# Half of an output projection computed in 32 steps among the steps of the samples' attention

## The chip, the core and the metric

One core of one Trainium2 chip. The time is device microseconds of one execution, median of three. The engines are PE (TensorE; PEld is its weight load), ACT (ScalarE), DVE (VectorE), POOL (GpSimd) and SP (SyncE, which here only issues DMAs). Each runs its own list of instructions in order, and they wait for each other on semaphores.

## The reference

One layer for 512 prompt tokens (one sequence) and 64 sample tokens (8 samples of 8 new tokens, each over 2048 cached positions). Attention has three branches, each with its own K and V; a short gated convolution stands beside it. Cut to what matters here:

```python
q, kv_c, kv_s, kv_w, gates, xin, bg, cg = in_projection(x, w_in)
attn = nsa_attention(...)         # gates0*o_cmp + gates1*o_sel + gates2*o_win
conv_out, conv_state = short_conv(xin, bg, cg, conv_prev, conv_w)
mix = concatenate([attn, conv_out]) @ w_out          # 2048 x 2048
h = layer_norm(ALPHA * x + mix, ln1_g, ln1_b)
f = square(relu(h @ w_mlp1)) @ w_mlp2
y = layer_norm(ALPHA * h + f, ln2_g, ln2_b)
```

The products with `w_out` are wanted for all 576 tokens. A token's row of `mix` depends on that token alone, so prompt tokens can be projected before the samples' attention is done.

## The kernel before

Activations lie transposed: 16 tiles of 128 features by T = 576 tokens, in two halves of TH = 288. The first half holds the prompt tokens 0 to 287, the second the other prompt tokens and the 64 sample tokens. The order of all work is written out by hand, engine by engine.

A float32 product is made of three passes: each operand is split into a high part (ACT's copy to `F32R`) and a low part (DVE's subtraction), and PE adds high x high, high x low and low x high. So one 128x128 block of a weight against one half of the tokens costs three matmuls of 288 columns.

The stages around the change, in order of time:

- the prompt's attention, up to about 795 us.
- The samples' attention, 795 to 993 us, one step for each of 8 samples. For sample b the cached K/V rows of the selected branch come in two gathers of 2 MB (`sg`, issued by POOL, one descriptor of 16 KB for each row), those of the window in one load of 1 MB (`wb`, SP). There are six chunks of keys: 0 and 1 in the first gather, 2 and 3 in the second, 4 the window, 5 the new tokens. `k_turn` transposes a chunk on PE, ACT copies it to `kT` (L914), `k_qk` makes the scores (L2257, chunk 5 L2259), DVE adds the mask (L1525, L1529) and takes the maxima (L1540). While the keys of sample b are worked on, sample b-1 is finished: ACT's exponentials (`s_exp`, L919), DVE's scaling (L1558), transposes of the weights (`s_turn`, L2270), ACT's copy to `sT` (L929), products with V (`s_pvs`, L2292), and `o_turn` (L2299) with DVE's addition to `mix`. A buffer of `sg` may be refilled when its products with V are done; there are four. There are two `kT`.
- The output projection, 996 to 1214 us, in two passes over the same weights. Pass 0 is for the first half of the tokens, pass 1 for the second. In each pass, for each of the 16 output tiles, SP loads a 1 MB weight tile (five DMAs), ACT makes its high part (L794), DVE its low part (L799), PE runs 48 matmuls (`gemm_half`, L2344), and DVE adds the residual from `x_scratch` (`residual`, L1613 and L1615) and adds up the sum for the layer norm. The tokens' own splits are made ahead of pass 0 for both halves (L969, L1604), tile by tile, and the first `gemm_half` waits for each.
- Beside pass 1, the layer norm of the first half; then the MLP.

## Time and profile before

| | |
|---|---|
| median of 3 runs | 2720.15 us (2719.93, 2720.15, 2726.3) |
| profiled execution, span from first to last instruction | 2725.8 us |
| PE busy | 2605.0 us, 96% of the span |
| DVE busy | 2001.9 us, 73% |
| ACT busy | 1073.5 us, 39% |
| HBM read and written | 385.53 MB and 96.80 MB |

### The profile page before, as it was taken

Reading aid. Unit: us, or ns where it says so; the run is one execution under the profiler, and the core shown is the slowest. Engines: PE = TensorE matmul, PEld = TensorE weight load, DVE = VectorE, ACT = ScalarE, POOL = GpSimd, SP = SyncE. Lnnn points to the kernel's source line nnn. Section 1 sums busy time; section 2 is a strip of 40 time slices with the busy share of each in tenths; the row PEclk is TensorE's granted clock in tenths of the full one; section 3 lists DMA queues with packets and bytes.
Section 4 is the critical chain, followed back from the end, with each engine's and each line's share of the span. In section 5 each row is a group of like instructions: output and inputs, shape, how many; then the busy total and the mean of one; then the engine's idle time right before and its main releaser. Section 6 shows DMA issues by size and latency. Waiting matters only on the chain.

```text
span 2725.8 us, 52530 instructions
## 1 busy us (share of the span) xinstructions
PE 2605.0 (96%) x20061; PEld 2482.8 (91%) x20061; DVE 2001.9 (73%) x3169; ACT 1073.5 (39%) x1349; POOL 66.6 (2%) x118
## 2 busy tenths in 40 slices
PE   8999999998888889996999999999999999999998
PEld 8999999995556569996999999999999999999997
DVE  5778732326864455689888888888888888888898
ACT  3111111116764453455555555555533333333333
POOL 1000000000001100000000000000000000000001
PEclk9999999998999999998999999999999999999999
DMA  8776643316025547653555555555796556555642
GB/s 263 229 242 209 184 77 77 87 39 236 2 94 221 210 135 210 197 157 116 190 188 194 193 192 189 185 190 190 255 321 190 180 168 209 184 186 177 201 125 85
DMA packets 510464, 475.35 MB, mean 174 GB/s; under 512 B 48957, under 2 KB 460885, under 8 KB 499447
## 3 DMA queue, kind: packets, MB, share of 16 engines
q1 hardware_dynamic: 505306, 406.85, 47.7%
q0 software_dynamic: 4736, 67.18, 6.5%
q8 instruction: 59, 0.97, 0.2%
q14 instruction: 31, 0.25, 0.0%
q10 hardware_dynamic: 332, 0.11, 0.0%
HBM read 385.53 MB, written 96.80 MB: 177 GB/s over the span
## 4 chain that ended last, share of the span: by engine, by line
PE 63%; DVE 5%; DMA 3%; issue 2%; ACT 2%; SPq 1%; DVEq 0%; ACTq 0%; POOL 0%; POOLq 0%
PE ps L2432 49%; PE ps L2344 6%; PE ps L2292 1%; DMA sg<-in_cache_slc,idx 1%; PE ps L2191 1%; PE ps L2244 1%; PE ps L2181 1%; DMA f_b<-f_scratch 1%; DVE pS L1473 1%; PE ps L2257 1%; PE ps L2270 1%; PE ps L2205 1%; DVE o_rows L1987 0%; DVE w_sl L1630 0%; ACT pT L895 0%
## 5 line engine op out<-in xcount | busy, mean ns | idle before, releaser
L1027 ACT ACTIVATE w_sh<-w_s 128x1024 fp32r<-128x1024 f32 (+1 forms) x512 | 473.5, 949 | 785.5 <-PE ps L2432 522.2
L2432 PE MATMUL ps<-f_b,w_sh 128*128 128x288 f32 x3584 | 714.5, 296 | 10.1 <-DMA f_b<-f_scratch 7.7
L1630 DVE TENSOR_TENSOR w_sl<-w_s,w_sh 128x1024 fp32r<-128x1024 f32 (+1 forms) x512 | 554.7, 1089 | 124.3 <-ACT w_sh L1027 124.1
L2432 PEld LDWEIGHTS ps<-f_b,w_sh 128*128 128x128 f32 x3584 | 574.2, 189 | 13.4 <-DMA f_b<-f_scratch 7.5
L2432 PE MATMUL ps<-f_b,w_sl 128*128 128x288 f32 x1792 | 527.0, 294 | 0.0
L2432 PE MATMUL ps<-h_u,w_sh 128*128 128x288 f32 x2560 | 514.3, 296 | 11.4 <-DVE h_u L1770 10.9
L2432 PEld LDWEIGHTS ps<-h_u,w_sh 128*128 128x128 f32 x2560 | 411.1, 189 | 12.9 <-issue 6.8
L2432 PE MATMUL ps<-h_u,w_sl 128*128 128x288 f32 x1280 | 376.7, 294 | 0.0
L794 ACT ACTIVATE w_hi<-w_raw 128x2048 fp32r<-128x2048 f32 x77 | 147.6, 1917 | 554.3 <-PE ps L2032 466.3
L2432 PEld LDWEIGHTS ps<-f_b,w_sl 128*128 128x128 f32 x1792 | 338.9, 189 | 0.0
L2032 PE MATMUL ps<-x_hi,w_hi 128*128 128x288 f32 x1408 | 302.6, 297 | 0.0
L2032 PE MATMUL ps<-x_hi,w_lo 128*128 128x288 f32 x1408 | 301.2, 296 | 0.0
L2032 PE MATMUL ps<-x_lo,w_hi 128*128 128x288 f32 x1408 | 300.9, 295 | 0.0
L2432 PEld LDWEIGHTS ps<-h_u,w_sl 128*128 128x128 f32 x1280 | 242.5, 189 | 0.0
L2032 PEld LDWEIGHTS ps<-x_hi,w_lo 128*128 128x128 f32 x1408 | 226.5, 189 | 0.0
L2032 PEld LDWEIGHTS ps<-x_lo,w_hi 128*128 128x128 f32 x1408 | 226.5, 189 | 0.0
L2032 PEld LDWEIGHTS ps<-x_hi,w_hi 128*128 128x128 f32 x1408 | 226.3, 189 | 0.1
L2432 PE MATMUL ps<-h_a,w_sh 128*128 128x288 f32 x1024 | 208.4, 296 | 13.5 <-DVE w_sl L1630 13.5
L799 DVE TENSOR_TENSOR w_lo<-w_raw,w_hi 128x2048 fp32r<-128x2048 f32 x77 | 176.6, 2293 | 60.6 <-ACT w_hi L794 58.8
L1882 DVE TENSOR_TENSOR y_t<-y_t,ps 128x288 f32 (+1 forms) x416 | 182.7, 450 | 45.5 <-PE ps L2432 43.2
L2344 PE MATMUL ps<-mixs,w_hi 128*128 128x288 f32 x1024 | 208.7, 299 | 5.3 <-DVE mixs L1604 3.2
L2432 PEld LDWEIGHTS ps<-h_a,w_sh 128*128 128x128 f32 x1024 | 164.8, 189 | 13.8 <-DVE w_sl L1630 13.7
(302 smaller groups left out, 3153.1 us busy)
## 6 DMA issues: line engine op xcount, KB each, us to landing
w_s<-in_w_mlp SPq DMA_DIRECT2D x512, 256.0 KB, 3.7
f_scratch<-f_st SPq DMA_DIRECT2D x32, 2016.0 KB, 8.9
f_b<-f_scratch SPq DMA_DIRECT2D x56, 1152.0 KB, 8.3
w_raw<-in_w_in SPq DMA_DIRECT2D x90, 512.0 KB, 5.1
w_raw<-in_w_out SPq DMA_DIRECT2D x128, 128.0 KB, 2.9
w_raw<-in_w_out SPq DMA_DIRECT2D x32, 512.0 KB, 4.3
x_r<-x_scratch SPq DMA_DIRECT2D x32, 288.0 KB, 4.4
wb<-in_cache_win SPq DMA_DIRECT2D x8, 1024.0 KB, 7.6
```

Source lines behind the costliest of these rows:

```text
L794: nc.scalar.activation(w_hi[s % 2][:, :], w_raw[s % 2][:, :], ACT.Copy).then_inc(s_hi, 1)
L799: nc.vector.tensor_tensor(w_lo[s % 2][:, :], w_raw[s % 2][:, :], w_hi[s % 2][:, :].bitcast(F32), ALU.subtract).then_inc(s_lo, 1)
L1027: nc.scalar.activation(w_sh[m][:, :, :], blocks, ACT.Copy).then_inc(z_h[m], 1)
L1473: last = nc.vector.tensor_tensor_reduce(pS[u % 4][:, br, 0:n], ps[:, 2 * (u % 2) + br, 0:n], causal[:, TP - n:TP], -1.0, 3e38, ALU.add, AL ...
L1630: nc.vector.tensor_tensor(w_sl[m][:, :, :], blocks, w_sh[m][:, :, :].bitcast(F32), ALU.subtract).then_inc(z_l[m], 1)
L1882: nc.vector.tensor_tensor(view, view, ps[:, bank, 0:TH], ALU.add).then_inc(z_e[m], 1)
L2032: last = nc.tensor.matmul(out[:, h, :], w[:, k * P:(k + 1) * P], x[:, k, h * TH:(h + 1) * TH], start=(k == 0 and m == 0), stop=(k == KT - ...
L2181: last = nc.tensor.matmul(ps[:, 2 * gl + br, 0:n], pq[a][half, n - P:n], kv_t[half, kv + a, 0:n], start=True, stop=True)
L2191: last = nc.tensor.transpose(ps[:, 4 + x // 4, (x % 4) * P:(x % 4 + 1) * P], pS[u % 4][:, br, kt * P:(kt + 1) * P], ident[:, :])
L2205: last = nc.tensor.matmul(ps[gl * HD:(gl + 1) * HD, 6 + a, i * P:(i + 1) * P], kvn[:, kt, v0:v0 + HD], pT[(2 * j + gl + 16 * r) % 3][:, x, ...
L2344: last = nc.tensor.matmul(ps[:, 2 * (s % 2), 0:TH], w[:, k * P:(k + 1) * P], mixs[:, p, x, k, :], start=(k == 0 and m == 0), stop=(k == KT ...
L2432: last = nc.tensor.matmul(ps[:, bank, 0:TH], w[b][:, at_, cols], acts(k, x), start=(start and n == 0), stop=(stop and n == 2), skip_group_ ...
```

## The change

Pass 0 is taken out of the projection and cut into 32 parts (`e_part`, `e_step`), which stand on PE among the steps of the samples' attention. Part e belongs to output tile e // 2. Even parts take the 8 feature tiles of the convolution, odd parts the 8 of the attention, so a part is 24 matmuls of 288 columns, and the weight comes in half tiles of 512 KB (`e_load`: one DMA for an even part, four for an odd one), with its own splits (`e_split` on ACT, `e_low` on DVE, 128x1024 each). Two parts stand in step 0, four in each of the steps 1 to 7, two behind them. The result of a tile (with the residual, `e_residual`) goes to memory (`c_scratch`, `e_store`), and before the layer norm it is read back into `h_t` in four DMAs. The splits of the first half of the tokens (`mix_high`, `mix_low`, 4 pieces of 128x1152) are made in step 0; those of the second half stay behind the attention. Pass 1 keeps its 16 tiles of 48 matmuls.

To make room, `sg` has three buffers where there were four, and `kT` and its two banks of PSUM are single where they were double. From sample 1 on the chunks come in the order 0, 1, 4, 2, 3, 5. The loops over samples are written out.

The core of the diff:

```diff
-S_OUT2 = S_OUT + KT
-S_MLP = S_OUT2 + KT
+S_MLP = S_OUT + KT
...
+NE = 2 * KT
+E_FIRST = (0,) + tuple(2 + 4 * n for n in range(NB))
+FIRST_CHUNKS, CHUNKS = (0, 1, 2, 3, 4, 5), (0, 1, 4, 2, 3, 5)
...
+        m_hi = at("m_hi", X0, [P, KT, TH], F32R)
+        m_lo = at("m_lo", C0, [P, KT, T], F32R)
+        sg = [at(f"sg{i}", X0 + HB + 16384 * ((i + 1) % 3), [P, GROW, ROWW]) for i in range(3)]
+        assert X0 + HB + 3 * 16384 <= B0
...
+        kT = at("kT", B0 + 14400, [P, 2, 512])
+        e_xr = at("e_xr", B0 + 18496, [P, 2, TH])
+        sT = [at(f"sT{i}", B0 + 22592 + 2048 * i, [P, 4, P]) for i in range(3)]
...
+            def e_load(e):
+                n, dst = slice(e // 2 * P, e // 2 * P + P), e_raw[e % 2]
+                if e >= 2:
+                    sp.wait_ge(e_los, e - 1)
+                if e % 2 == 0:
+                    sp.dma_start(dst[:, :].rearrange("p (k n) -> p k n", n=P), w_cnv_v[:, :, n]).then_inc(e_w[0], 16)
+                else:
+                    for a in range(2):
+                        for gl in range(2):
+                            sp.dma_start(dst[gl * HD:(gl + 1) * HD, :].rearrange("p (r a n) -> p r a n", r=R, a=2)[:, :, a, :],
+                                         w_att_v[a, gl][:, :, n]).then_inc(e_w[1], 16)
+            def e_load_x(n):
+                if n:
+                    sp.wait_ge(e_tile, 32 * n)
+                    sp.wait_ge(l_sum, 1 + n)
+                sp.dma_start(e_xr[:, :, :], x_dram[:, n, :, 0:TH]).then_inc(e_tile, 16)
+            def e_store(n):
+                sp.wait_ge(e_acc, 2 * n + 2)
+                sp.dma_start(c_dram[:, n, :], e_xr[:, 0, :]).then_inc(e_tile, 16)
+            sp.wait_ge(s_xsave, 16 * 2 * KT // 4)
+            e_load(0)
+            e_load(1)
+            load_window(0)
+            e_load_x(0)
+            load_window(1)
+            e_load(2)
+            e_load(3)
+            for b in range(1, NB):
...
+                e = E_FIRST[b]
+                e_load(e + 2)
+                e_store(e // 2 - 1)
+                e_load_x(e // 2)
+                e_load(e + 3)
+                e_load(e + 4)
+                e_store(e // 2)
+                e_load(e + 5)
+                e_load_x(e // 2 + 1)
+                if b + 1 < NB:
+                    load_window(b + 1)
...
+            e_store(KT - 1)
+            load(S_OUT + 2, out_loads(S_OUT + 2, 1, 0))
+            load_x(2, 0)
+            sp.wait_ge(e_tile, 32 * KT)
+            sp.wait_ge(s_mlo, 4 + KT)
+            sp.wait_ge(e_mm, NE)
+            for q in range(4):
+                sp.dma_start(h_t[:, 4 * q:4 * q + 4, 0:TH], c_dram[:, 4 * q:4 * q + 4, :]).then_inc(e_tile, 16)
+            load(S_OUT + 3, out_loads(S_OUT + 3, 1, 1))
+            load_x(3, 0)
...
+            def seq_gather(m):
+                if m >= 3:
+                    pool.wait_ge(t_pv, 6 * ((m - 3) // 2) + 2 * ((m - 3) % 2) + 2)
+                nc.gpsimd.tensor_copy(idx1[m % 4][:, :], idx[:, m:m + 1]).then_inc(s_idx1, 1)
+                pool.wait_ge(s_idx1, 2 * NGATH + 2 * m + 1)
+                pool.sem_inc(s_idx1, 1)
+                nc.gpsimd.indirect_dma_start(
+                    sg[m % 3][:, :, :].rearrange("p j c -> p (j c)"), None, slc_rows,
+                    bass.IndirectOffsetOnAxis(ap=idx1[m % 4][:, 0:1], axis=0)).then_inc(s_sg[m % 3], 16)
...
+            def e_split(e):
+                act.wait_ge(e_w[e % 2], (64 if e % 2 else 16) * (e // 2 + 1))
+                if e >= 2:
+                    act.wait_ge(e_mm, e - 1)
+                nc.scalar.activation(e_high(e)[:, :], e_raw[e % 2][:, :], ACT.Copy).then_inc(e_his, 1)
...
+            mix_high(0)
+            k_copy(0, 0)
+            mix_high(1)
+            k_copy(0, 1)
+            mix_high(2)
+            e_split(0)
+            k_copy(0, 2)
+            mix_high(3)
+            e_split(1)
+            k_copy(0, 3)
+            k_copy(0, 4)
+            e_split(2)
+            e_split(3)
+            for b in range(1, NB):
+                e = E_FIRST[b]
+                k_copy(b, 0)
+                s_exp(b - 1)
+                k_copy(b, 1)
+                e_split(e + 2)
+                for g in range(3):
+                    p_copy(b - 1, g)
+                k_copy(b, 2)
+                e_split(e + 3)
+                p_copy(b - 1, 3)
+                p_copy(b - 1, 4)
+                k_copy(b, 3)
+                if b < NB - 1:
+                    e_split(e + 4)
+                    e_split(e + 5)
+                k_copy(b, 4)
+                p_copy(b - 1, 5)
+                if b == NB - 1:
+                    e_split(e + 4)
+                    e_split(e + 5)
+                o_copy(b - 1)
...
+            def e_low(e):
+                dve.wait_ge(e_his, e + 1)
+                nc.vector.tensor_tensor(e_lo[e % 2][:, :], e_raw[e % 2][:, :], e_high(e)[:, :].bitcast(F32), ALU.subtract).then_inc(e_los, 1)
+            def e_residual(n):
+                dve.wait_ge(e_mm, 2 * n + 2)
+                dve.wait_ge(e_tile, 32 * n + 16)
+                nc.vector.scalar_tensor_tensor(e_xr[:, 0, :], e_xr[:, 0, :], ALPHA, ps[:, 2 + n % 2, 0:TH], ALU.mult, ALU.add).then_inc(e_acc, 1)
+                dve.wait_ge(e_acc, 2 * n + 1)
+                nc.vector.scalar_tensor_tensor(e_xr[:, 0, :], e_xr[:, 1, :], ALPHA, e_xr[:, 0, :], ALU.mult, ALU.add).then_inc(e_acc, 1)
+                dve.wait_ge(e_acc, 2 * n + 2)
+                dve.wait_ge(l_sum, n + 1)
+                nc.vector.tensor_tensor(h_sum[:, 0:TH], h_sum[:, 0:TH], e_xr[:, 0, :], ALU.add).then_inc(l_sum, 1)
...
+            mix_low(0)
+            mix_low(1)
+            k_scores(0, 0)
+            mix_low(2)
+            k_scores(0, 1)
+            mix_low(3)
+            e_low(0)
+            k_scores(0, 2)
+            e_low(1)
+            k_scores(0, 3)
+            k_scores(0, 4)
+            k_scores(0, 5)
+            k_max(0)
+            e_low(2)
+            e_residual(0)
+            for b in range(1, NB):
+                e = E_FIRST[b]
+                if b > 1:
+                    s_out_add(b - 2)
+                e_low(e + 1)
+                s_scale(b - 1)
+                k_scores(b, 0)
+                k_scores(b, 1)
+                e_low(e + 2)
+                k_scores(b, 2)
+                e_residual(e // 2)
+                e_low(e + 3)
+                k_scores(b, 3)
+                if b < NB - 1:
+                    e_low(e + 4)
+                k_scores(b, 4)
+                k_scores(b, 5)
+                k_max(b)
+                if b == NB - 1:
+                    e_low(e + 4)
+                e_residual(e // 2 + 1)
...
+            def e_part(e, j0, j1):
+                n, kh = e // 2, e % 2
+                if j0 == 0:
+                    pe.wait_ge(e_los, e + 1)
+                    if kh == 0 and n >= 2:
+                        pe.wait_ge(e_acc, 2 * n - 3)
+                    if n == 0:
+                        pe.wait_ge(s_mlo, 2 * kh + 2)
+                for j in range(j0, j1):
+                    k, cols = j if kh else NCONV + j, slice(j * P, (j + 1) * P)
+                    hi, lo = e_high(e)[:, cols], e_lo[e % 2][:, cols]
+                    for m, (w, x) in enumerate(((hi, m_hi[:, k, :]), (hi, m_lo[:, k, 0:TH]), (lo, m_hi[:, k, :]))):
+                        last = nc.tensor.matmul(ps[:, 2 + n % 2, 0:TH], w, x, start=(kh == 0 and j == 0 and m == 0),
+                                                stop=(kh == 1 and j == 7 and m == 2))
+                if j1 == 8:
+                    last.then_inc(e_mm, 1)
...
+            k_turn(0, 0)
+            k_turn(0, 1)
+            k_qk(0, 0)
+            k_turn(0, 2)
+            k_qk(0, 1)
+            e_step(0)
+            k_turn(0, 3)
+            k_qk(0, 2)
+            e_step(1)
+            k_turn(0, 4)
+            k_qk(0, 3)
+            k_qk(0, 4)
+            k_qk(0, 5)
+            for b in range(1, NB):
+                e = E_FIRST[b]
+                k_turn(b, 0)
+                if b > 1:
+                    o_turn(b - 2)
+                e_step(e)
+                k_qk(b, 0)
+                k_turn(b, 1)
+                s_turn(b - 1, 0)
+                s_turn(b - 1, 1)
+                k_qk(b, 1)
+                s_pvs(b - 1, 0)
+                s_turn(b - 1, 2)
+                s_pvs(b - 1, 1)
+                k_turn(b, 2)
+                e_step(e + 1)
+                k_qk(b, 2)
+                s_turn(b - 1, 3)
+                s_pvs(b - 1, 2)
+                s_turn(b - 1, 4)
+                s_pvs(b - 1, 3)
+                e_step(e + 2)
+                k_turn(b, 3)
+                e_step(e + 3)
+                k_qk(b, 3)
+                k_turn(b, 4)
+                s_turn(b - 1, 5)
+                s_pvs(b - 1, 4)
+                k_qk(b, 4)
+                s_pvs(b - 1, 5)
+                k_qk(b, 5)
+            o_turn(NB - 2)
+            e_step(NE - 2)
+            for g in range(6):
+                s_turn(NB - 1, g)
+                if g:
+                    s_pvs(NB - 1, g - 1)
+            s_pvs(NB - 1, 5)
+            e_part(NE - 1, 0, 4)
+            o_turn(NB - 1)
+            e_part(NE - 1, 4, 8)
...
-            for u in range(2):
-                gemm_half(S_OUT + u, 0, 0, ready=True)
-            with pe.Fori(1, KT // 2) as i:
-                for u in range(2):
-                    gemm_half(S_OUT + u, 2 * i, 0)
+            pe.wait_ge(e_acc, 2 * KT - 3)
             for i in range(8):
-                gemm_half(S_OUT2 + i, 0, 1)
+                gemm_half(S_OUT + i, 0, ready=i < 1)
```

ACT in the later part of a middle step of the attention, before. `kT` is the copy of transposed keys, `sT` that of transposed weights of the sample before, `o_sb` its result:

```order
L914 ACTIVATE kT_137<-ps 128x1024
L926 REGISTER_ALU
L929 ACTIVATE sT<-ps 128x512
L926 REGISTER_ALU
L929 ACTIVATE sT<-ps 128x512
L911 REGISTER_ALU
L912 REGISTER_ALU
L914 ACTIVATE kT_138<-ps 128x1024
L925 REGISTER_ALU
L926 REGISTER_ALU
L931 ACTIVATE sT<-ps 8x256
L936 ACTIVATE o_sb_144<-ps 128x128
```

The same part of a step in the changed kernel. `e_hi` is the high part of a half tile of `w_out`:

```order
L993 ACTIVATE kT<-ps 128x1024
L986 ACTIVATE e_hi_144<-e_raw_142 128x1024
L1012 ACTIVATE sT_138<-ps 128x512
L1012 ACTIVATE sT_139<-ps 128x512
L993 ACTIVATE kT<-ps 128x1024
L986 ACTIVATE e_hi_143<-e_raw_141 128x1024
L986 ACTIVATE e_hi_144<-e_raw_142 128x1024
L993 ACTIVATE kT<-ps 128x1024
L1014 ACTIVATE sT_140<-ps 8x256
L1019 ACTIVATE o_sb_154<-ps 128x128
```

The copies come in the order they had, with splits of weights between them, each of which waits for its own load; the last two stand ahead of the last `kT`. One more split stands earlier in the step, ahead of the first `sT`.

SP in the same step, before: one window and its two rows of new V, nothing else.

```order
L503 DMA wb_132<-in_cache_win 128x2048
L506 ISA
L506 DMA vn_136<-out 8x256
L506 ISA
L506 DMA vn_136<-out 8x256
```

And now, from the first half tile of a step to the next window:

```order
L535 DMA e_raw_141<-in_w_out 128x8x128
L552 DMA c_scratch<-e_xr 128x288
L547 DMA e_xr<-x_scratch 128x2x288
L539 DMA e_raw_142<-in_w_out 64x4x128 x4
L535 DMA e_raw_141<-in_w_out 128x8x128
L552 DMA c_scratch<-e_xr 128x288
L539 DMA e_raw_142<-in_w_out 64x4x128 x4
L547 DMA e_xr<-x_scratch 128x2x288
L525 DMA wb_130<-in_cache_win 128x2048
```

Every store waits for DVE's residual, every load of `e_xr` for the store ahead of it to land, and the window for the last product with V of the sample two before it.

## Rows read from the trace of the kernel before

**Rows 1.** The page, whole execution: span, and TensorE (busy, share, instructions).
```profile
span 2725.8 us, 52530 instructions
...
PE 2605.0 (96%) x20061; PEld 2482.8 (91%) x20061; DVE 2001.9 (73%) x3169; ACT 1073.5 (39%) x1349; POOL 66.6 (2%) x118
```

**Rows 2.** Busy time by stretch: PE, PEld, DVE, ACT, POOL, PEclk, DMA share, GB/s.
```profile
795.00:811.00 16.00, 11.80 (x76) 6.67 (x72) 7.71 (x17) 5.01 (x5) 3.39 (x7) 0.92 0.83 313
811.00:835.00 24.00, 21.68 (x178) 14.86 (x178) 9.11 (x23) 10.96 (x15) 2.52 (x5) 0.91 0.50 196
...
931.00:955.00 24.00, 21.68 (x183) 14.92 (x179) 10.35 (x30) 11.23 (x16) 2.45 (x5) 0.93 0.57 216
955.00:975.00 20.00, 15.92 (x107) 10.40 (x105) 10.65 (x30) 9.38 (x13) 0.00 (x0) 0.91 0.26 100
975.00:996.00 21.00, 15.45 (x194) 11.63 (x188) 7.39 (x23) 11.75 (x20) 0.00 (x0) 1.00 0.21 57
```

**Rows 3.** The chain of waits in one sample step: start us, us, what.
```profile
885.11 1.72 PE ps L2244 x8
...
887.85 1.07 ACT sS L919
...
894.14 1.02 PE ps L2292 x16
895.17 1.02 PE ps L2244 x8
896.19 1.01 PE ps L2257 x4
...
904.70 0.70 DVE sS L1529
...
905.52 1.05 PE ps L2259 x8
```

**Rows 4.** Busy time around that step's start, granted clock after POOL's column.
```profile
880.00:883.00 3.00, 2.11 (x20) 1.38 (x16) 1.63 (x5) 0.00 (x0) 0.21 (x1) 1.00 0.90 360
883.00:887.00 4.00, 4.00 (x23) 3.49 (x21) 1.28 (x7) 1.37 (x3) 0.19 (x1) 0.57 0.98 367
887.00:907.00 20.00, 17.68 (x162) 11.25 (x158) 9.11 (x23) 9.86 (x14) 2.53 (x5) 1.00 0.52 190
```

**Rows 5.** Timeline after a group of transposes, with the idle time before the next group.
```profile
896.12 0.20 PEld L2257 LDWEIGHTS ps<-kT,qb 128*64 128x64 f32 x4 [0.17 <-issue]
```

**Rows 6.** Products of the projection alone (L2344): PE, PEld, clock, DMA, GB/s.
```profile
996.00:1008.40 12.40, 10.64 (x49) 8.20 (x49) 0.86 0.86 231
1008.40:1105.00 96.60, 96.17 (x719) 95.94 (x720) 1.00 0.74 209
```

**Rows 7.** Groups of instructions by line, projection and attention stretch.
```profile
L914 ACT ACTIVATE kT<-ps 128x1024 f32<-128x1024 f32 x40 | 40.8, 1022 | 48.8 <-PE ps L2244 48.8
...
L1613 DVE SCALAR_TENSOR_TENSOR h_t<-x_r,ps 128x288 f32 x16 | 7.3, 454 | 30.5 <-PE ps L2344 30.5
```

**Rows 8.** The same view of the MLP stretch, for tiles of the new sizes.
```profile
L1630 DVE TENSOR_TENSOR w_sl<-w_s,w_sh 128x1024 fp32r<-128x1024 f32 x383 | 468.1, 1222 | 115.4 <-ACT w_sh L1027 115.2
...
L1027 ACT ACTIVATE w_sh<-w_s 128x1024 fp32r<-128x1024 f32 x383 | 403.4, 1054 | 381.0 <-DVE w_s L1653 252.6 <-PE ps L2432 120.4 <-DVE w_s L1635 5.5
...
L1770 DVE TENSOR_TENSOR h_u<-h_r,h_u 128x1152 fp32r<-128x1152 f32 x8 | 10.9, 1358 | 2.5 <-ACT h_u L1079 1.7
...
L1079 ACT ACTIVATE h_u<-h_r 128x1152 fp32r<-128x1152 f32 x8 | 9.3, 1164 | 16.2 <-DVE h_r L1762 16.2
```

**Rows 9.** DMA queues from 36 to 40 us: packets, MB, share of 16 engines.
```profile
q0 software_dynamic: 104, 1.70, 100.1%
q1 hardware_dynamic: 36, 0.01, 1.3%
```

**Rows 10.** Landing times of the two w_raw loads issued at 29.1 and 29.5.
```profile
DMA to landing us min/median/max: 5.4/10.0/14.6
```

**Rows 11.** The selection gathers (tile sg), 16 of them.
```profile
DMA to landing us min/median/max: 8.1/9.2/19.2
```

**Rows 12.** DMA issues of the output projection, KB each, median us to landing.
```profile
w_raw<-in_w_out SPq DMA_DIRECT2D x31, 512.0 KB, 4.3
```

More of the change, by code:

```diff
@@ L396, in build @@
         z_f = [sem(f"z_f{m}") for m in range(7)]
-        o_tr, o_cp = sem("o_tr"), [sem(f"o_cp{i}") for i in range(2)]
+        o_tr, o_cp = sem("o_tr"), sem("o_cp")
         s_dve, s_pool = sem("s_dve"), sem("s_pool")
@@ L542, in _ @@
                     sp.wait_ge(s_acc, 2 + S_OUT + n + 1 - XR + XR * i)
-                    load_x(n, i, 0)
-            with sp.Fori(0, KT // XR) as i:
-                for n in range(XR):
-                    load(S_OUT2 + n, out_loads(S_OUT2 + n, 2 * i + n // 2, n % 2), it=XR * i)
-                    sp.wait_ge(s_acc, 2 + S_OUT2 + n + 1 - XR + XR * i)
-                    load_x(n, i, 1)
+                    load_x(n, i)
             w1_v = w_mlp1[0].rearrange("(c k a p) n -> p c a k n", p=P, a=2, k=CK)
@@ L774, in _ @@
+            seq_gather(0)
+            seq_gather(1)
             pool.wait_ge(s_pv, 2 + UNITS)
             pool.wait_ge(s_of, 2 + 2 * R)
-            seq_q(0, 0)
-            seq_q(1, 0)
-            seq_gather(1, 0)
-            with pool.Fori(1, NB // 2) as i:
-                for h in range(2):
-                    seq_q(h, i)
-                    seq_gather(h, i)
+            seq_q(0)
+            seq_q(1)
+            seq_gather(2)
+            for b in range(1, NB):
+                seq_gather(2 * b + 1)
+                if b + 1 < NB:
+                    seq_gather(2 * b + 2)
+                    seq_q(b + 1)
@@ new lines, in _ @@
+            s_exp(NB - 1)
+            p_copy(NB - 1, 0)
+            p_copy(NB - 1, 1)
+            p_copy(NB - 1, 2)
+            act.wait_ge(e_los, NE)
+            split_hi(act, S_OUT)
+            for g in range(3, 6):
+                p_copy(NB - 1, g)
+            o_copy(NB - 1)
+            act.wait_ge(t_of, NB)
+            for k in range(0, KT, 2):
+                nc.scalar.activation(mixs[:, 0, k:k + 2, :], mix[:, k:k + 2, TH:T], ACT.Copy).then_inc(s_mhi, 2)
+            act.wait_ge(e_mm, NE)
@@ new lines, in _ @@
+            s_out_add(NB - 2)
+            e_low(NE - 1)
+            s_scale(NB - 1)
+            split_lo(dve, S_OUT)
+            s_out_add(NB - 1)
+            for k in range(0, KT, 2):
+                if k == 8:
+                    e_residual(KT - 1)
+                dve.wait_ge(s_mhi, 4 + k + 2)
+                nc.vector.tensor_tensor(mixs[:, 1, k:k + 2, :], mix[:, k:k + 2, TH:T], mixs[:, 0, k:k + 2, :].bitcast(F32),
+                                        ALU.subtract).then_inc(s_mlo, 2)
@@ L2208, in p_pv @@
                             last.then_inc(s_pv, 1)
-            for first in (t_qk, t_pv, t_pt):
-                pe.sem_inc(first, 12)
             pe.sem_inc(s_qk, 1)
```

377 lines of the change are left out of this document (150 added, 227 removed).

## The prediction

> **What bounds the kernel now.** I read the page first: PE is busy for 2605.0 of 2725.8 us [rows 1]. All matmuls that pass 0 needs are still run, so nothing shortens PE's own work: the change can only put products where PE stands idle. The busy times by stretch [rows 2] say where that is. The samples' attention goes from 795 to 996 us; its first step takes 16.0 us with PE busy for 11.8, the next six 24.0 us each with PE busy for 21.7 (the first and the last of them are shown; DVE has 9 to 10 and ACT 11 of the 24), and the last two stretches 41.0 us with 31.4. That is 4 + 14 + 10 = 28 us of idle PE, the most that the parts could fill there. Next I read the chain of one such step [rows 3]. It is mostly PE, with short links through ACT and DVE: the exponentials (1.07 on the chain), the window's scores (0.70). Two groups of 8 transposes take 1.72 us at its start, and the same group takes 1.02 later [rows 3]. The busy times around them say why: the granted clock is 0.57 over 4 us, so 1.2 GHz for about 3.4 of them, after 3 us in which PE was busy for 2.1; then it is back at 1.00 [rows 4]. This costs 2 x 0.7 = 1.4 us in each step. So a step is 24.0 = 20.3 of work, 1.4 of clock, 2.3 of waits. The last view is that of the products alone [rows 6]: 720 in 96.6 us, 0.134 each, and the first 48 in 12.4 us instead of 6.4, since they wait for the splits of the tokens.
>
> **What moves, and its break-even.** A part is 24 x 0.134 = 3.2 us of PE, the four of a step 12.9. Pass 0 shrinks by exactly that. So a middle step must take less than 24.0 + 12.9 = 36.9 us, or the move costs.
>
> **Middle steps (1 to 6).** PE: 20.3 + 12.9, and each part is one more group with a join. A join shows as 0.17 us of idle PEld between two groups whose operands are long there [rows 5]; I take 0.15, so 0.6 for four. Sum 33.8. On top of it:
> - Clock. What stands at the end of a step is what stood there before: the last scores of 512 columns, the scores of the new keys, the short products, and a wait. I take it that the clock falls as it did. But now a dense part stands behind it, so half speed for 3.4 us costs 1.7 instead of 1.4. Bounds: 0, if the parts keep the clock up, and 3.4, if it falls twice.
> - Waits. DVE gets four `e_low` of 1.22 [rows 8] and six instructions of 0.46 [rows 7], 7.6 us, to its 10; ACT four splits of 1.05, 4.2 us, to its 11. Both stay under 20 of 37 us and cost nothing by their sum. What costs is the order on ACT, where a split waits for a load and copies that PE needs stand behind it. The loads are pieces of 512 bytes, and gathers of 16 KB pieces run beside them in every step. Where they met before, the gather took the DMA engines: in 4 us 104 packets with 1.70 MB of its queue, and 36 packets with 0.01 MB of the other [rows 9]; the load issued 1 us ahead of two gathers landed after 14.6 us, its neighbour after 5.4 [rows 10]. Now the fourth load of a step (`e_load(e + 5)`) is issued about 22 us into the step, when DVE has made the low part ahead of it, and the second gather is asked for at the same place, after the fourth product with V. A gather lands after 9.2 us [rows 11], and about 1 us passes before it is issued, so both are there at about 33. ACT then splits (1.05) and copies `kT` (1.02 [rows 7]): about 35.2. PE, with the clock's 1.7, wants that copy at 33.8 + 1.7 - 2.7 = 32.8. A wait of 2.4. This takes the place of the 2.3 that the step had, which the parts do fill. Bounds: 0.5 (load ahead of the gather) to 8 (another of the loads stands behind a gather too).
> - The gather with three buffers. Between the product with V that frees a buffer and the chunk that needs it PE has two groups of keys, two of scores and products with transposes and two parts, 3.4 each, in all 11.6 us (groups of 1.02 and transposes of four at half of that [rows 3]); the gather needs 1 + 9.2: hidden, with 1.4 to spare. Above 10.6 us of landing it shows; the slowest took 19.2 [rows 11], beside other traffic.
>
> So 33.8 + 1.7 + 2.4 = 37.9 against 36.9: +1.0, six times, **+6.0**.
>
> On this the Trainium skill has two rules. "TensorE: Matmul & The Clock Gate", section "Loop structure matters more than you think": matmuls that stand back to back stay warm. Rows 4 show only that the clock fell behind thinner work; by the rule the parts would hold it up, and a step would be 36.2, a saving of 0.7. "DMA: Bandwidth & Descriptors", section "Queues, rings and completion order": a DMA engine takes the queues in turn, by packets. Rows 9 agree, and the rule speaks against the change: with pieces of 512 bytes against 16 KB a turn each is next to nothing, and it holds for every load that meets a gather.
>
> **Step 0.** Before, 16.0 us [rows 2]. Now ACT has the four splits of the tokens (1.16 each, DVE's half 1.36 [rows 8]) and two of weights among its copies, and the first part waits for them. By the order: ACT three token splits, two `kT` and the first weight split, 3 x 1.16 + 2 x 1.02 + 1.05 = 6.6; then `kT` 1.02 and the last token split 1.16; DVE 1.36 and 1.22; part 0, 3.2; two groups of PE, 2.0; scores and maximum, 1.4; the second `e_low` 1.22; part 1, 3.2; two groups, 2.0; the only `kT`, 1.0; the last scores, 1.0 + 0.7 + 1.05. That is 29.1 us, with some fifteen links of 0.1 30.6, and I take 31, since the first half tiles are loaded beside a gather and two windows. Bounds: 28, and 36. 31 - 16.0 - 6.4 = **+8.6**. This is the step that speaks most against the change: two parts bring 6.4 us of work into a step of 16 and lengthen it by 15.
>
> **The end.** Before, 41.0 us from the last sample's keys to the first product [rows 2]. Now step 7: 33.8 + 1.7 + 0.5, as there is no next gather. Then part 30 (3.4), which hides the exponentials but not DVE's scaling (some 3 more), six pairs of transposes and products with V (9.0), part 31 (3.2), and the splits of the second half (1.4): 20.0. Together 56.0, less six parts (19.3) 36.7: **-4.3**. The first tile of pass 1: its token splits are in pieces half as large in all, DVE's 8 x 0.75 and a residual, so about 9.0 instead of 12.4: **-3.4**. Then the way back from memory: 2.36 MB are read ahead of the fourth weight tile. In the projection 209 GB/s are moved at a share of 0.74 [rows 6], so 282 at the most: 8.4 us for it and 3.7 for each 1 MB tile. From the last store, about 7 us into pass 1: 3.7 + 8.4 + 3.7 and both splits (4.2) is 27; the fourth tile's products are due at 9.0 + 2 x 6.4 = 21.9. **+5.4**; bounds 0 and 10. A tile alone lands in 4.3 [rows 12], so the later ones catch up. Sum of the end: -2.3. Storing and loading the tiles in the steps costs PE nothing more; SP waits there, not PE.
>
> **Sum.** 8.6 + 6.0 - 2.3 = +12.3 us. Against the profiled execution that is 2725.8 + 12.3 = 2738.1 of span; against the median, 5.65 lower, 2720.15 + 12.3 = **2732**.
>
> **The rivals.**
> - A: faster. The parts keep the clock up and the late load comes in time: a step is 33.8 + 0.5 = 34.3, -2.6 six times, -15.6; step 0 at 29.5, +7.1; the end without clock and with half of the wait for memory, -2.3 - 1.7 - 2.7 = -6.7. Sum -15: 2705. For it: idle of 2.3 in each step is there to fill, and DVE and ACT have room. Against it: rows 9 and 10.
> - B: no difference that can be told. Only one of the two holds. Clock up, load late: 36.2, -0.7 six times, -4.2, + 8.6 - 4.0 = 0: 2720. Load in time and the clock down: 36.0, -5.4 + 8.6 - 2.3 = +1: 2721.
> - C: much slower. Each of the loads that stand ahead of copies meets a gather, above all the second of a step, ahead of the fourth `sT`, and slows the gather in turn beyond its 1.4 us to spare. A step of 33.8 + 1.7 + 7 = 42.5, +5.6 six times, 33.6 + 8.6 - 2.3 = +40: 2760. It decides from the point where the load of part e + 3 lands later than about 18 us into the step. For it: rows 10. Against it: this load is issued some 3 us before the first gather is.
> - D: the change does nothing: parts stand in PE's list beside the waits, not in them. 24.0 + 12.9 + 0.6 = 37.5, +3.6 + 8.6 - 2.3 = +10: 2730. It can't be told from the forecast by time, only by the waits before `kT` and `sT`.
>
> **How the numbers follow.** A run of this kernel tells about 0.3% from no change, 8.2 us: below 2712.0 is faster, above 2728.3 slower. Chances: forecast and D together 0.42 (2724 to 2741), A 0.18, B 0.24, C 0.16. Of the forecast's case a tenth of the chance, 0.04, falls within 0.3%; of A one in six, 0.03, does; of B 0.03 lies above. Faster 0.16, the same 0.27, slower 0.57. The range leaves out the far half of A and of C: 2705 to 2758; the likeliest case alone 2724 to 2741. The sum has no term that could be large and favourable at once: idle PE is 28 us in all, and the clock takes 9 more.
>
> **What would show it.** Step 0 of 31 us, with the first part waiting for a low part of DVE. Middle steps of 37.9 with one wait of 2 to 3 us ahead of the last 512-column scores, released by `kT`, and that by the split of the fourth half tile, and that by its DMA, landing after 8 us or more while others take 4 to 5. The granted clock at half once in a step. 12.9 us less of pass 0 for each. The fourth tile of pass 1 late by 5 us. I am wrong if middle steps are under 36 us, or if the clock stays at 1.00 through the attention.

## The result and the profile after

The changed kernel takes 2761.43 us (median of 4, 2759.07 to 2762.6), the kernel before 2722.52 (median of 4, 2719.93 to 2726.3). The ratio is 1.0137, 95% interval 1.0122 to 1.0151: slower by 39 us, where 12 were forecast. The time lies 3 us above the range of 2705 to 2758.

The page's first lines, of the profiled execution (2760.63 us; they answer to [rows 1]):

```profile
span 2758.8 us, 51737 instructions
...
PE 2626.6 (95%) x20061; PEld 2500.7 (91%) x20061; DVE 2005.2 (73%) x3181; ACT 1072.8 (39%) x1361; POOL 70.2 (3%) x118
```

The span is 33 us longer and PE is busy for 21.6 of them, with the same 20061 matmuls: some of them run slower. The busy times by stretch, as in [rows 2] (step 0, steps 1, 2 and 5, then step 7 and the end):

```profile
795.00:831.20 36.20, 23.66 (x119) 16.66 (x117) 15.82 (x18) 13.11 (x13) 2.60 (x4) 0.79 0.54 183
831.20:872.10 40.90, 37.26 (x275) 29.20 (x276) 18.70 (x38) 15.02 (x20) 3.19 (x5) 0.88 0.56 178
872.10:913.80 41.70, 37.30 (x277) 29.68 (x277) 18.10 (x39) 15.01 (x20) 3.18 (x5) 0.87 0.63 200
995.80:1036.50 40.70, 36.88 (x276) 29.25 (x277) 18.10 (x39) 15.02 (x20) 3.18 (x5) 0.88 0.63 204
1077.10:1133.30 56.20, 52.50 (x436) 43.51 (x436) 28.13 (x67) 24.59 (x35) 1.14 (x2) 0.92 0.46 144
```

A middle step is 41.0 us (246.0 for six), where 36.9 would break even. DVE and ACT are busy for 18 and 15 of them, so neither is the bound. The mean clock fell to 0.88, where [rows 2] have 0.91 to 0.93. The budget against the forecast, each difference net of the parts moved (24 x 0.134 = 3.22 us each); the numbers taken off are the stretch before (15.8 and 143.9 us) and the parts:

| | forecast | measured |
|---|---|---|
| step 0 | +8.6 | 36.1 - 15.8 - 6.4 = +13.9 |
| steps 1 to 6 | +6.0 | 246.0 - 143.9 - 77.2 = +24.9 |
| the end, up to the MLP | -2.3 | -1.9 |
| ahead of step 0 and after the MLP's start | 0 | -3.7 |
| sum | +12.3 | +33 |

What gave the last 3.7 us back was not looked into.

The chain of waits at the end of step 4 (start us, us, what) names the wait:

```profile
976.38 1.15 DVE e_lo L1628
...
979.51 9.55 DMA e_raw<-in_w_out
...
989.20 0.85 issue
990.05 1.01 ACT kT L993
991.06 0.04 issue
991.11 1.97 PE ps L2401 x4
993.08 1.05 PE ps L2441 x8
994.13 1.81 PE ps L2403 x8
995.93 1.80 PE ps L2385 x8
```

This is the forecast's chain link by link: DVE's low part, the load of `e_load(e + 5)`, ACT's split (the 0.85 of "issue" are its first part), the `kT` copy, and PE. The instructions of SP, ACT and POOL there, and what ended ACT's idle time:

```profile
977.54 2.59 SPq L539 DMA_DIRECT2D e_raw<-in_w_out  x4
...
978.37 0.96 POOL L834 DMA_INDIRECT sg<-in_cache_slc,idx  x1 [0.81 <-POOLq L833]
...
989.09 1.06 ACT L986 ACTIVATE e_hi<-e_raw 128x1024 fp32r<-128x1024 f32 x1 [6.02 <-DMA e_raw<-in_w_out]
990.05 1.00 ACT L993 ACTIVATE kT<-ps 128x1024 f32<-128x1024 f32 x1
```

Then the groups in the chain take too long: eight transposes 1.80 us against the 1.02 of [rows 3], the 512-column scores 1.97 against 1.01. The busy times around them, granted clock third from the end:

```profile
986.00:990.00 4.00, 1.50 (x21) 1.02 (x19) 1.82 (x2) 0.91 (x1) 0.00 (x0) 1.00 0.55 129
990.00:1000.30 10.30, 9.19 (x40) 7.26 (x41) 4.92 (x14) 4.12 (x6) 0.00 (x0) 0.50 0.50 156
1000.30:1008.00 7.70, 7.02 (x56) 4.78 (x55) 5.83 (x16) 4.13 (x8) 0.00 (x0) 1.00 0.44 123
```

The clock is at its lower level, 1.2 GHz, for 10.3 us, where [rows 4] have it there for 3.4. All six middle steps have such a stretch of 10.2. What it costs, from start to start of the groups against the same groups at full clock: scores 1.90 against 1.01, short products 1.05 against 0.86, the new keys' scores 1.73 against 0.91, transposes 1.74 against 0.91, the first part 4.80 against 3.34. That is 0.89 + 0.19 + 0.82 + 0.83 + 1.46 = 4.2 us a step. At the wait itself two matmuls start 3.2 to 4.0 us apart (3.5 in the mean of the six steps), which start 0.15 apart where nothing is waited for: 3.3 more. Together 7.5 us a step.

### The profile page after: what moved, and what is told of

It is laid out like the page before. It is cut to its first block, busy times and chain, and to the rows that moved or that the text cites. A ratio compares the mean times of both kernels' runs of the same rounds, so it can differ in the third digit from the quotient of the medians.

```text
span 2758.8 us, 51737 instructions
## 1 busy us (share of the span) xinstructions
PE 2626.6 (95%) x20061; PEld 2500.7 (91%) x20061; DVE 2005.2 (73%) x3181; ACT 1072.8 (39%) x1361; POOL 70.2 (3%) x118
## 4 chain that ended last, share of the span: by engine, by line
PE 62%; DVE 6%; DMA 3%; ACT 3%; issue 2%; SPq 1%; DVEq 0%; ACTq 0%
PE ps L2620 49%; PE ps L2536 3%; PE ps L2463 3%; DMA e_raw<-in_w_out 2%; PE ps L2401 1%; PE ps L2331 1%; PE ps L2385 1%; PE ps L2441 1%; PE ps L2321 1%; DVE pS L1575 1%; PE ps L2345 1%; DMA f_b<-f_scratch 1%; PE ps L2403 0%; DVE o_rows L2127 0%; DVE w_sl L1775 0%
## 5 line engine op out<-in xcount | busy, mean ns | idle before, releaser
L2620 PE MATMUL ps<-h_u,w_sh 128*128 128x288 f32 x2560 | 516.3, 297 | 10.3 <-DVE h_u L1910 9.9
L861 ACT ACTIVATE w_hi<-w_raw 128x2048 fp32r<-128x2048 f32 x61 | 116.8, 1915 | 483.9 <-PE ps L2172 466.3
L866 DVE TENSOR_TENSOR w_lo<-w_raw,w_hi 128x2048 fp32r<-128x2048 f32 x61 | 139.9, 2294 | 53.2 <-ACT w_hi L861 51.4
L1786 DVE TENSOR_TENSOR w_s<-w_s 128x1024 f32<-128x1024 f32 x128 | 156.5, 1223 | 2.3
```

What stands on the lines that cost most here:

```text
L861: nc.scalar.activation(w_hi[s % 2][:, :], w_raw[s % 2][:, :], ACT.Copy).then_inc(s_hi, 1)
L866: nc.vector.tensor_tensor(w_lo[s % 2][:, :], w_raw[s % 2][:, :], w_hi[s % 2][:, :].bitcast(F32), ALU.subtract).then_inc(s_lo, 1)
L1786: nc.vector.tensor_tensor(w_s[:, b + 2:SUM_2 + 1:SUM_2 - b - 2, :], w_s[:, b + 2:SUM_1 + 1:SUM_1 - b - 2, :], w_s[:, b:b + 1, :].broadcast ...
L2620: last = nc.tensor.matmul(ps[:, bank, 0:TH], w[b][:, at_, cols], acts(k, x), start=(start and n == 0), stop=(stop and n == 2), skip_group_ ...
```

## The experiments

The theory after this: one late load per step makes one wait, and that wait, through the clock, costs twice its length. Its rivals: the clock falls because of what PE does at a step's end, whatever it waits for; the load is late for some reason other than the gather. In each expectation "1, 2, 3" are its own theories.

**The late split moved.** In steps 1 to 6:

```diff
                 if b < NB - 1:
                     e_split(e + 4)
-                    e_split(e + 5)
                 k_copy(b, 4)
...
                 o_copy(b - 1)
+                if b < NB - 1:
+                    e_split(e + 5)
```

> ACT's split of the fourth half tile (e + 5) stands behind the copy of o(b-1) in place of ahead of kT(b, 4), in steps 1 to 6; nothing else is changed. Theory 1 (the late load makes the wait of 3.9 us ahead of the last keys' scores, and that wait makes the clock stay at half for 10.2 us a step in place of 3.4): the wait goes and the clock is down for about 3.4 us, a step goes from 41.0 to about 36.0 us (33.8 + 1.7 + 0.5), 6 x 5 = 30 less, 2731 us. Theory 2 (the clock falls because of the thin groups at a step's end, whatever is waited for): only the wait goes, some 3.4 us a step, the half clock stays at about 10 us, 2741 us. Theory 3 (the split only hands its wait on to the first kT of the next step): no gain, within 5 us of 2761.

Measured: 2716.74 us, ratio to before 0.9956 (0.994 to 0.9973), 44.7 below the changed kernel (which ran beside other runs of the kernel before; by the two ratios it is 49). One line moved on ACT, and the kernel is faster than before. A step of it:

```profile
969.60:1003.10 33.50, 32.41 (x277) 26.03 (x276) 18.07 (x41) 15.14 (x20) 3.19 (x5) 1.00 0.76 248
```

The clock is at 1.00 from 838 to 1070 us. The wait and the low clock went together, and the step fell by 7.5 us where the first theory expected 5. Theories 2 and 3 are out.

**The same, and a part put into the gap.** `e_step(e + 3)` stands between `s_pvs(b - 1, 4)` and `k_qk(b, 4)`, the split late as above.

> The late split of the first experiment, and besides PE's part e + 3 stands between the last short products with V of b-1 and the last keys' scores of b, in place of after the transposes of chunk 3, in steps 1 to 6. If the half clock comes from thin groups and the wait at a step's end, a dense group of 3.2 us there covers both: 1 to 2.6 us a step below the first experiment, 2717 to 2725 us. If the wait is already gone and the clock falls at the same place anyway: the same time as the first experiment within 3 us. Rival: the gap that the part leaves ahead of the scores of chunk 3 becomes a wait of its own (kT copy or exponentials), 1 us a step, 6 us slower than the first experiment.

Measured: 2727.89 us, ratio 1.0006 (0.9996 to 1.0016). The last rival came true: steps of 34.96, since the part no longer covers the copy of chunk 3's keys:

```profile
963.51 1.02 ACT L993 ACTIVATE kT<-ps 128x1024 f32<-128x1024 f32 x1 [4.68 <-PE ps L2386]
```

PE's transposes for this copy start at their pace, and then the next group 2.15 us later instead of 0.79. A part where it stood hid exactly such a link. This wait of 1.4 us did not lower the clock.

**Only PE's wait, made by hand.** Loads and gathers as in the first experiment; ACT makes `e_split(e + 4)`, ahead of `kT(b, 4)`, in 64 pieces of 16 columns, later in 80 pieces (64 of 8 columns and 16 of 32):

```diff
-                    e_split(e + 4)
+                    e_split(e + 4, 64)
```

> As the first experiment (split of the fourth half tile late, steps of 33.5 us, clock up), but ACT makes the split of the third half tile (e + 4), ahead of kT(b, 4), in 64 pieces of 16 columns; no load and no gather is changed. Pieces that start 0.1 us apart take 6.4 us in place of 1.0; ACT had 3.2 us of idle time there, so PE should wait 2 to 4 us at the place where it did in the changed kernel. If PE's wait alone brings the half clock, it is down for 3.4 to 10 us behind it, and a step takes the wait and 1.5 to 4.3 us more: 37 to 41 us, 2738 to 2762. If the half clock needs something of the late load or the gather, the step takes only the wait more, the clock stays at 1.00: 35.5 to 37.5 us, 2729 to 2741.

> As the experiment with 64 pieces (PE waited 2.4 us there, half clock for 3.4 us, a step of 37.55), but the split of the third half tile is in 80 pieces: some 1.8 us more on ACT, a wait of about 4.2. No load and no gather is changed. If the length of the wait is what stretches the half clock (10.2 us in the changed kernel behind waits of 3.2 to 4.0), it is down for 10.2 us and a step takes 33.5 + 4.2 + 4 = 41.7: 2764 to 2768. If the long half clock needed the load beside the gather, it stays at 3.4 us and a step takes 39.3: 2750 to 2752.

Measured with 64 pieces: 2740.37 us, ratio 1.0057 (1.0042 to 1.0072). A step, and the 3.4 us of half clock that it has once:

```profile
905.80:943.30 37.50, 34.30 (x276) 27.57 (x276) 18.15 (x40) 20.68 (x83) 3.19 (x5) 0.96 0.69 222
...
941.40:944.80 3.40, 3.40 (x18) 3.40 (x18) 2.84 (x12) 1.48 (x3) 0.00 (x0) 0.51 0.91 316
```

Measured with 80 pieces: 2765.32 us, ratio 1.0142 (1.0123 to 1.0161). A step, the wait, and what follows it:

```profile
915.00:956.20 41.20, 36.72 (x278) 29.10 (x277) 18.21 (x40) 22.17 (x99) 3.18 (x5) 0.87 0.63 202
945.70:948.00 2.30, 0.28 (x6) 0.03 (x2) 0.00 (x0) 2.30 (x24) 0.00 (x0) 0.99 0.53 108
948.00:958.20 10.20, 8.43 (x37) 6.50 (x38) 5.99 (x15) 4.96 (x13) 0.00 (x0) 0.50 0.43 138
```

So a wait of PE is enough, with no DMA in it, and either cost about 1.7 to 2 times its own length. No wait: 33.5 us, clock up. Two matmuls that start 2.57 us apart at the wait: half clock for 3.4 us, 37.55. 4.07 apart: 10.2 us in five of the six stretches (6.8 in one), steps of 40.0 to 41.8, 41.2 in the mean. 1.5 us more on ACT, which is busy for 22 of 41 us, cost 3.6 us a step. The changed kernel (3.2 to 4.0 apart) behaves like the longer one, with a DMA in place of the pieces. That the length alone decides is not so, as the next kernel shows.

**Why the load is late: its bytes.** The half tiles from the third on are read as one block of four or eight, so most weights of these parts are left out:

```diff
-  dst..."p (k n) -> p k n"...,             w_cnv_v[:, :, n]
+  dst..."p (k n) -> p k n"...[:, 0:1, :],  w_cnv_v[:, 0:1, n]
```

> The half tiles of weights from the third on are loaded as one block of each in place of all (as many DMAs, a fraction of their 512-byte pieces), so most of the weights of these parts are left out; all waits, splits and products stay. Theory 1 (a load of small pieces that meets the gather gets next to nothing of the DMA engines): the fourth load of a step lands in some 3 to 5 us in place of 9.6, the wait ahead of the last keys' scores goes and the half clock shortens to 3.4 us, steps of about 36 us, 2731 us, step 0 as before. Theory 2 (the load is late for where it stands on its queue or for the gather's own time, not for its bytes): it lands as late as with all its bytes, and steps stay within 1 us of 41.0, 2761 us. Clock theory 2: wait gone, half clock for 10 us all the same, 2741 us.

Measured: 2747.18 us, ratio 1.0067 (1.0051 to 1.0084), 14 below the changed kernel, with waits of 2.2 to 3.6 us between two matmuls and steps of 37.0 to 41.4. With a quarter of its pieces the load was hardly earlier (SP, then POOL, then ACT, in one step):

```profile
969.24 2.39 SPq L542 DMA_DIRECT2D e_raw<-in_w_out  x4
...
970.06 0.96 POOL L837 DMA_INDIRECT sg<-in_cache_slc,idx  x1 [0.81 <-POOLq L836]
...
980.50 1.06 ACT L989 ACTIVATE e_hi<-e_raw 128x1024 fp32r<-128x1024 f32 x1 [5.75 <-DMA e_raw<-in_w_out]
```

Landed 11.2 us after its first issue, against 11.5 in the changed kernel. Neither theory had it as it is. The queues of this kernel from 972 to 977 us, and of the changed kernel from 982.5 to 985.5, show what moved beside the gather (packets, MB, share of the 16 engines):

```profile
q0 software_dynamic: 99, 1.62, 81.7%
q1 hardware_dynamic: 98, 0.04, 3.0%
```

```profile
q0 software_dynamic: 74, 1.21, 94.4%
q1 hardware_dynamic: 59, 0.03, 3.3%
```

Once the gather is under way, and until its last us, about one small packet or fewer, most of them 512 bytes, moves for one of 16 KB. A gather has 128 of the large ones (2 MB in rows of 16 KB). Of the whole load's 1024 pieces 393 moved ahead of the gather's first packet, 48 in the four us from 981 to 985, and most of the rest from 986 us on, when the gather's packets were over. This accounts for the whole load. It does not account for the small one: of its 256 pieces 128 moved ahead of the gather's first packet, 124 beside it and 4 behind, and still its last completion came at 980.48 us, just behind the gather's at 980.29. The Trainium skill, "DMA: Bandwidth & Descriptors", section "Queues, rings and completion order", has engines take the queues in turn by packets; 98 to 99 agrees with turns of one piece each, the 59 to 74 here and the 36 to 104 of [rows 9] only roughly. The same section says that a completion signal lands only after every earlier write of its DMA engine, across queues. The small load that came no earlier fits that, but no run here separates it from the turns.

This kernel also tells what the length of PE's wait leaves out. All matmuls are there, and the waits stand at the same place. Two of them, with the half clock that came with each:

```profile
PE ps L2404 <- ACT kT L996: 2.3, 1, 2.3
906.90:910.30 3.40, 3.40 (x17) 3.40 (x16) 3.22 (x12) 1.82 (x2) 0.00 (x0) 0.51 0.93 331
```

```profile
PE ps L2404 <- ACT kT L996: 2.0, 1, 2.0
941.10:951.30 10.20, 10.18 (x44) 8.24 (x45) 5.31 (x17) 4.01 (x6) 0.00 (x0) 0.50 0.35 128
```

The shorter wait has the longer half clock. What differs is when the granted clock fell from 1.00 to 0.50: 3.0 us behind the end of the first wait, inside the second. The middle steps of the changed kernel, of the ones with 64 and 80 pieces and of this one have 24 such waits:

| the clock fell | times | two matmuls apart by | half clock |
|---|---|---|---|
| inside the wait | 13 | 2.2 to 4.1 us | 10.2 us each time |
| 0.5 to 1.5 us behind its end | 3 | 2.4 to 4.1 | 6.8 |
| 2.7 to 3.0 us behind its end | 8 | 2.3 to 2.6 | 3.4 |

A longer wait was more often still on when the clock fell; what sets the moment of the fall no run here shows.

**Why the load is late: the gather.** The changed kernel in its own order, but POOL waits for the load before it issues the second gather:

```diff
                 if b + 1 < NB:
+                    pool.wait_ge(e_w[1], 64 * ((E_FIRST[b] + 5) // 2 + 1))
                     seq_gather(2 * b + 2)
```

> The changed kernel in its own order (the fourth split ahead of kT(b, 4)), but the second gather of a step is issued only when all pieces of the fourth half tile have landed. Theory: the load alone lands in 3 to 4 us (as the odd load of part e + 3 does, 3.2), so the split comes in time, no wait ahead of the last keys' scores, clock up: steps of 33.5 to 35, if the gather, some 3 us later, still lands before its chunk; 2717 to 2725. Rival 1: the gather's landing becomes the wait in place of the load's: 1 to 3 us a step and the half clock with it, steps of 36 to 40, 2731 to 2755. Rival 2: the load lands as late as before (it isn't the gather): steps over 41, later than 2761.

Measured: 2736.37 us, ratio 1.0045 (1.0031 to 1.0059). Rival 1 came true. Without this gather beside them the four pieces landed 2.7 to 3.8 us after their issues, and the wait ahead of the last keys' scores is gone. In its place:

```profile
966.61 0.18 POOL L831 COPY idx<-idx 128x1 uint32<-128x1 uint32 x1 [12.92 <-DMA e_raw<-in_w_out]
967.60 0.96 POOL L834 DMA_INDIRECT sg<-in_cache_slc,idx  x1 [0.81 <-POOLq L833]
...
PE ps L2386 <- DMA sg<-in_cache_slc,idx: 2.2, 2, 1.8
```

The gather lands 8.3 us after 967.60, and PE's next keys stood still for 1.8 us: steps of 36.1 to 37.9, with half clock for 3.4 us in five of six. The waits of this kernel (two matmuls 1.8 to 3.1 us apart) stand ahead of transposes with a part soon behind them, and none of them came with more than 3.4 us. So it is the gather beside it that makes the load late, and load and gather do not both fit ahead of PE one after the other. Splitting late lets both run at once.

**Step 0.** Three orders of it. First only copies and scores ahead of the splits and both parts at the end; then, besides, the window loaded first on SP; last, both splits of half tiles behind the fifth `kT` copy, on top of the first experiment:

```diff
-            k_turn(0, 2); k_qk(0, 1); e_step(0); k_turn(0, 3); k_qk(0, 2); e_step(1); ...
+            k_turn(0, 2); k_qk(0, 1); k_turn(0, 3); k_qk(0, 2); ...; k_qk(0, 5); e_step(0); e_step(1)
```

> Only step 0 is written in another order: kT copies and scores stand ahead of the splits of tokens on ACT and DVE, and both parts stand at the end of the step. Theory (step 0 took 36.1 us because its first part waits for six splits and the kT copies of the keys stand behind them): step 0 takes 25 to 28 us, 8 to 11 less, 2751 to 2753 us. Rival (the parts' splits simply hold up step 1, or the half clock of three times 6.8 us in this step is what costs): under 3 us gained over steps 0 and 1 together, 2758 to 2761 us.

> The order of the third experiment in step 0 (copies and scores of keys first, both parts at the end), and besides SP loads the first window ahead of the first two half tiles. In the third experiment the part began at the same place as before because the window's transposes waited 6.0 us for their rows. If those stood behind the 1 MB of half tiles, the wait goes and step 0 takes 25 to 28 us in place of 35.3, with it the half clock behind that wait: 8 to 10 us below the third experiment, 2750 to 2752. Rival: the two gathers hold the window back wherever it stands on its queue; then the window's chunk waits 4 us or more as before and the time is within 3 us of 2760.

> The first experiment (fourth split late) and step 0 in another order again: ACT makes all five kT copies of sample 0, with the splits of the tokens between them, ahead of both splits of half tiles; DVE's low parts likewise; both parts stand at the end; the first window is loaded first. In the last kernels the fifth kT copy stood 5 to 6 us behind a split that waited for its half tile. Theory: the keys of sample 0 then end after some 19 us, the parts take 6.4 and a split's 1 us, step 0 about 27 us in place of 35.6: 8 us below the first experiment, 2709. Rival: the half tiles land so late beside gather and windows (they landed 14 us into the step at worst) that the first part starts at 821 as ever: within 2 us of 2717.

Measured: 2760.06 us (ratio 1.0117, 1.01 to 1.0134), 2757.92 (1.0114, 1.0098 to 1.0129), and 2709.03 (0.9938, 0.9919 to 0.9957). In the first two, taken by themselves, the parts began at 821.5 and 822.5 us, as the second did in the changed kernel (821.10). What PE waited for ahead of the window's keys, in the first, and what ACT waited for, in the second (us in total, times, longest):

```profile
PE ps L2385 <- DMA vn<-out: 6.0, 1, 6.0
```

```profile
ACT e_hi L986 <- DMA e_raw<-in_w_out: 6.6, 2, 6.0
```

Whichever of window and half tile came later on SP's queue was there late: the window's transposes began at 812.6 us in the first, the split at 810.9 in the second, and a copy that PE needs stood behind it. Half clock came with it in both (13.7 us of it in the second). With the splits behind the copies nothing of the keys waits for a half tile, and step 0 is 27.5 us. This is the fastest kernel of the case, 8 us below the first experiment, as expected. Its step 0 with the group ahead of it, and a middle step:

```profile
795.00:823.70 28.70, 20.86 (x140) 15.29 (x139) 17.17 (x25) 12.39 (x12) 1.82 (x4) 0.94 0.74 231
858.10:891.60 33.50, 32.41 (x277) 26.03 (x276) 18.06 (x40) 15.02 (x20) 3.18 (x5) 1.00 0.76 247
```

**The way back from memory.** The four reads of the summed tokens stand behind the fourth weight tile:

```diff
-            (four reads of h_t)
             load(S_OUT + 3, out_loads(S_OUT + 3, 1, 1))
+            (four reads of h_t)
```

> Only the four reads that bring the summed tokens back (2.36 MB) stand behind the fourth weight tile on SP's queue in place of ahead of it. Theory (they make this tile late by 5.4 us): its products come in time, the four tiles of pass 1 behind the first take 7.6 us each, 4 to 5 us less, 2756 to 2757. Rival (the reads then delay the later tiles or the mean's start as much as they did this one): no gain within 2 us of 2761.

Measured: 2762.75 us, ratio 1.013 (1.0114 to 1.0145): no gain. In the changed kernel the fourth tile is late:

```profile
PEld ps L2536 <- DVE w_lo L866: 5.7, 1, 5.7
```

With the reads later, the sums of squares over them are what PE waits for, and then the next tile's low part all the same:

```profile
DVE h_t L1819 <- DMA h_t<-c_scratch: 9.9, 1, 9.9
PEld ps L2549 <- ACT sqh L1085: 4.5, 2, 4.4
...
PEld ps L2536 <- DVE w_lo L866: 3.6, 1, 3.6
```

The rival came true. Both are due at the same time, and in these two orders one or the other was late.

**All edits together** (late split, the second order of step 0, the reads later):

> All four edits: the fourth half tile's split late, step 0 in the new order, the first window loaded ahead of the half tiles, the summed tokens read back behind the fourth weight tile. By their single sizes: 2716.7 - 9 - 4.5 = 2703. If the first kernel's gain is only there with a part between the keys of step 0, or if the read back still shows, 2708 to 2716. Rival: step 0 gains nothing, 2712.

Measured: 2718.04 us, ratio 0.9963 (0.9949 to 0.9976): the gain of the late split alone, for the two reasons above. The best kernel is the one with the late split and the third order of step 0, 2709.03.

## Why the prediction was wrong

- **What bounds it:** right. PE's idle time was there to fill, and what the forecast had as 33.8 us of work took 33.5 once nothing waited for long. No term of the work in these steps was mis-sized.
- **Middle steps, the wait:** right in place, in order of events and in cause; 2.4 us forecast, 3.2 to 4.0 from start to start measured, inside the bounds of 0.5 to 8. The load landed 9.55 us after its last issue, as the 9.2 of [rows 11] had it; its four pieces were issued 23.2 to 25.1 us into the step (the fourth) and not at 22. The "about 33" for the landing is not the sum of its own terms, 22 + 1 + 9.2 = 32.2; measured it was 34.7.
- **Middle steps, the clock: this step failed.** I took it "that the clock falls as it did", 1.7 us a step, with bounds of 0 and 3.4. It was 4.2. I added wait and clock as if they had nothing to do with each other. They have: with the wait gone the clock stayed up, with a wait alone it fell. The experiment with a wait of 2.57 us from start to start gave 37.55 us, near the forecast's 37.9 for a wait of 2.4; the one of 4.07 gave 41.2. Even a wait of the forecast's length can have the long half clock, as the one of 2.2 us had. The term's upper bound, two falls of 3.4 us, had no case with a fall that lasts. The middle steps of the kernel before show none, but its first step has one of 6.8 us and the MLP's start one of 10.2, behind waits of 2.8 and 6.9 us, and I took neither into account. They stand there in the kernel before, by the busy times:

```profile
808.30:815.10 6.80, 4.44 (x21) 3.99 (x23) 1.19 (x7) 1.19 (x2) 0.40 (x1) 0.50 0.86 366
...
1228.10:1238.30 10.20, 4.35 (x17) 4.03 (x17) 9.71 (x18) 7.57 (x13) 0.00 (x0) 0.50 0.43 173
```

  Six steps at 41.0 instead of 37.9 are 18.9 of the 20.7 us by which the span missed, and the clock's 2.5 more in each are 15 of them.
- **The rule on the clock.** I weighed the rule of the Trainium skill ("TensorE: Matmul & The Clock Gate", section "Loop structure matters more than you think"), that matmuls back to back stay warm, against "it falls as it did". With the late split the clock stays at 1.00 for 230 us, which agrees with the rule; the parts alone did not bring it about, since the experiments with 64 and 80 pieces have the same parts. What it needed was that the wait went.
- **The gather with three buffers:** right, hidden as long as it is issued where it was; issued later, behind the fourth load, it showed.
- **Step 0:** +13.9 against +8.6, with 36.1 us at the edge of the bounds of 28 to 36. The terms listed add up to 28.1 us and not 29.1, so with the links it should have said 29.6; the 31 had 1.4 us to spare and was short by 5 all the same. The links were as worked out (the first part waited 4.8 us for DVE's low part, the second 2.6), but the half clock of 15 us in it was in no term. The first two orders show that what is late there is the window or the half tile, whichever is loaded second; that the gather beside them is the reason was not tested for this step.
- **The end:** -1.9 against -2.3: 56.2 us to the first product (56.0), the first tile 8.3 (9.0), PE idle for 5.4 ahead of the fourth tile (5.4, though its terms, 27 and 21.9, give 5.1).
- **The rivals.** C gave 2760, the right time by the wrong way: the load of part e + 3 landed 3.2 us after its issue, well in time, and met no gather; only the fourth did. A's conditions (clock up, load in time) are what the late split made, and its steps of 34.3 came at 33.5.

## What to carry to other kernels

When a change fills an engine's idle time but leaves one wait of some microseconds in each turn of a loop, price that wait together with what the clock does in and behind it, and with bounds as wide as the longest stretch of half clock in the trace at hand: here 2.6 us between two matmuls cost 4 us a step in all, 4.1 cost 7.7, and waits of 2.2 to 2.6 us came with 3.4, 6.8 or 10.2 us of half clock. On an in-order engine put what waits for a DMA behind the copies that the bound engine needs, and a load of small pieces ahead of a gather of large ones or so early that it may take the gather's whole time. Look for the one late link before giving up a change: moving one line on ACT turned +39 us into -9.5, and another order of the first step besides into -16.5.

## What the runs showed of the hardware

- For the same work around the wait the time at half clock came in leaps of 3.4, 6.8 and 10.2 us. It was 10.2 in all 13 cases in which the clock fell inside the wait, with 2.2 to 4.1 us between two matmuls, and 3.4 in all 8 in which it fell 2.7 to 3.0 us behind it.
- The clock stayed up where the longest time between two matmuls was 1.4 us and parts stood around it (the part put into the gap), and fell for 3.4 us a step in the kernel before behind 1.4 to 1.5 us and thin work [rows 4].
- A load with a quarter of its 512-byte pieces landed as late beside a gather of 16 KB pieces as the whole one (11.2 and 11.5 us after its first issue), with one small packet moved per large one (98 and 99 in 5 us) or fewer (59 and 74 in 3); without that gather each DMA of the whole load took 2.7 to 3.8.
- A copy of 128x16 on ACT starts every 0.107 us (64 of them in 6.83), 6.5 times the 1.05 us of one copy of all 1024 columns.
